# A decoder block on one core: two more pairs of gate and up tiles made by seven half-size products, the sums for it made earlier and those for the down projection later

## The reference

```
h = rms_norm(x, norm1);  proj = h @ w_in
o_diff = differential attention (4 heads);  o_nsa = compressed + selected + window attention (8 heads)
x = x + concat(o_diff, rms_norm(o_nsa)) @ w_out
h = rms_norm(x, norm2)
x = x + (silu(h @ w_gate) * (h @ w_up)) @ w_down        # w_gate, w_up: 1024 x 2816, w_down: 2816 x 1024
return rms_norm(x, final_norm)
```

## Time and profile before

| | |
|---|---|
| median of 3 runs | 668.09 us (666.64 to 669.31) |
| the profiled execution, its own time | 663.55 us |
| its span in the trace | 661.7 us |
| PE busy | 646.4 us, 98% of the span |
| DVE, ACT, POOL busy | 457.0, 348.7, 264.4 us |
| full tiles, from the first later chunk to the pairs | until 428.51 us |
| pairs | 428.51 to 548.72 us |
| down | from 548.72 us |

### The profile page before, as it was taken

How to read it: one execution, slowest core, us unless ns; L and a number is a source line. 1 busy time by engine, 2 the same in 40 slices (tenths; PEclk the granted TensorE clock), 3 DMA queues, 4 the chain that set the end, 5 groups by cost and what they waited for, 6 DMA issues and landing times.

```text
span 661.7 us, 11056 instructions
## 1 busy us (share of the span) xinstructions
PE 646.4 (98%) x3915; PEld 569.6 (86%) x3915; DVE 457.0 (69%) x929; ACT 348.7 (53%) x689; POOL 264.4 (40%) x158
## 2 busy tenths in 40 slices
PE   8999999999999799999999999999999999999996
PEld 7988988898899687888878888899999998888884
DVE  5435446555655777634579987669888798788894
ACT  7546446688564358725332353344444446655663
POOL 4766253684242431134356766444444320000222
PEclk9999999999999999999999999999999999999999
DMA  8979959469794982044699999977677858756553
GB/s 251 264 180 257 280 147 243 131 183 375 206 254 126 251 157 65 1 153 127 158 306 281 298 279 298 245 215 213 198 228 213 253 180 264 257 198 197 186 171 127
DMA packets 114774, 139.22 MB, mean 210 GB/s; under 512 B 5044, under 2 KB 74784, under 8 KB 114720
## 3 DMA queue, kind: packets, MB, share of 16 engines
q1 hardware_dynamic: 97880, 107.35, 50.6%
q0 software_dynamic: 14176, 26.64, 22.5%
q10 hardware_dynamic: 2664, 4.53, 1.9%
HBM read 132.19 MB, written 54.81 MB: 283 GB/s over the span
## 4 chain that ended last, share of the span: by engine, by line
PE 92%; DVE 2%; issue 2%; ACT 1%; POOL 1%; DMA 1%; POOLq 0%; ACTq 0%; DVEq 0%
PE bank L795 10%; PE bank L797 9%; PE bank L796 9%; PE bank L776 9%; PE bank L778 9%; PE bank L777 9%; PE bank L1107 6%; PE bank L1105 6%; PE bank L1106 6%; PE bank L948 6%; PE bank L924 3%; PE bank L908 2%; PE bank L909 2%; PE bank L987 1%; DMA causal<-in_c_causal_dram 1%
## 5 line engine op out<-in xcount | busy, mean ns | idle before, releaser
L728 POOL TENSOR_TENSOR w_lo<-raw,w_hi 128x1024 fp32r<-128x1024 f32 (+1 forms) x76 | 192.9, 2542 | 265.0 <-ACT w_hi L1148 264.2
L1148 ACT CAST w_hi<-raw 128x1024 fp32r<-128x1024 f32 (+1 forms) x141 | 144.2, 1028 | 141.4 <-PE bank L1107 51.8
L795 PE MATMUL bank<-xT_hi,w_hi 128*128 128x512 f32 x272 | 108.9, 400 | 0.8 <-POOL w_lo L728 0.5
L797 PE MATMUL bank<-xT_hi,w_lo 128*128 128x512 f32 x272 | 107.0, 394 | 0.0
L796 PE MATMUL bank<-xT_lo,w_hi 128*128 128x512 f32 x272 | 106.8, 392 | 0.0
L1617 DVE CUSTOM_DVE_ANT_0 bank<-bank,bias 128x128 f32<-128x128 f32 (+3 forms) x96 | 47.6, 497 | 74.5 <-PE bank L909 45.5
L1774 DVE TENSOR_TENSOR w_lo<-raw,w_hi 128x1024 fp32r<-128x1024 f32 x66 | 78.0, 1182 | 28.0 <-ACT w_hi L1148 28.0
L1229 ACT ACTIVATE E<-bank,nmax 128x128 f32<-128x128 f32 (+3 forms) x80 | 42.4, 530 | 38.3 <-DVE nmax L1617 37.5
L795 PEld LDWEIGHTS bank<-xT_hi,w_hi 128*128 128x128 f32 x272 | 51.2, 188 | 11.9 <-issue 1.2
L797 PEld LDWEIGHTS bank<-xT_hi,w_lo 128*128 128x128 f32 x272 | 51.1, 188 | 11.7
L796 PEld LDWEIGHTS bank<-xT_lo,w_hi 128*128 128x128 f32 x272 | 51.3, 188 | 9.7 <-issue 0.2
(11 more groups left out here) (280 smaller groups left out, 1615.7 us busy)
## 6 DMA issues: line engine op xcount, KB each, us to landing
raw<-mixed_sums SPq DMA_DIRECT2D x24, 512.0 KB, 4.4
raw<-in_w_gate_dram SPq DMA_DIRECT2D x22, 512.0 KB, 7.5
raw<-in_w_in_dram SPq DMA_DIRECT2D x20, 512.0 KB, 6.0
down_sums<-in_w_down_dram SPq DMA_DIRECT2D x20, 512.0 KB, 10.4
raw<-down_sums SPq DMA_DIRECT2D x20, 512.0 KB, 4.1
raw<-in_w_up_dram SPq DMA_DIRECT2D x16, 512.0 KB, 4.5
raw<-in_w_down_dram SPq DMA_DIRECT2D x15, 512.0 KB, 3.3
mixed_sums<-in_w_up_dram SPq DMA_DIRECT2D x12, 512.0 KB, 10.9
```

Source lines behind the costliest of these rows:

```text
L728: nc.gpsimd.tensor_tensor(wv_lo(k)[:, 0:n], raw[:, k % RAW_SLOTS, 0:n], wv_hi(k)[:, 0:n].bitcast(F32), ALU.subtract).then_inc(s_split, 1)
L795: nc.tensor.matmul(bank[:, :], hi, xT_hi[:, kt, :], start=kt == 0, stop=False)
L797: return nc.tensor.matmul(bank[:, :], lo, xT_hi[:, kt, :], start=False, stop=kt == KT - 1)
L1148: nc.scalar.copy(wv_hi(k)[:, 0:n], raw[:, k % RAW_SLOTS, 0:n]).then_inc(s_whi, 1)
```

## The change

`F0` goes from 10 to 6, so that four tiles of gate and up leave stage 1 and become two more pairs of stage 2 (6 pairs before, 8 now). The sums for the pairs grow from 24 to 32, so there are 56 in all, and their places are set anew. The ring of result banks gets another order, since the bank that gate and up used last must not be wanted first. POOL's loop now runs over the chunks of the down projection too, where six sums are made, and in each round it starts its sums last.

```diff
-F0 = 10
+F0 = 6
@@ plan_sums
-    for wides in ((0, 1), (2,)):
+    for wides in ((0, 1), (2, 3)):
@@ hymba_block
-    copy_at = [6 + i for i in range(10)] + [27 + i // 2 for i in range(14)]
-    copy_at += [n_fill + i for i in range(20)] + [n_fill + 2 * F0 + 4 + 10 * i for i in range(4)]
-    add_at = copy_at[0:16] + [30, 30, 30, 30, 31, 31, 31, 31] + copy_at[24:]
+    mixed0, down_from = n_fill + 2 * F0, n_fill + 2 * F0 + N_UNIT * N_PAIR
+    copy_at = [6 + i for i in range(10)] + [27 + i // 2 for i in range(14)] + [36] * 4
+    copy_at += [n_fill + i for i in range(12)] + [mixed0 + 3 + 5 * i for i in range(10)] + [down_from + 8 + 3 * i for i in range(6)]
+    add_at = copy_at[0:16] + [31] * 8 + [33] * 4 + copy_at[28:]
@@
-        RING = [ps[0], ps[6], ps[3], ps[4], ps[5], ps[2], ps[7], ps[1]]
+        RING = [ps[3], ps[4], ps[5], ps[2], ps[0], ps[6], ps[7], ps[1]]
@@ gpsimd
-            for k in range(down0):
+            for k in range(len(chunks)):
                 if not by_dve[k]:
                     split(k)
-                for i in [i for i in range(len(todo)) if add_at[i] == k]:
-                    add_sum(i)
                 if k == LAMBDA_AFTER:
...
                 if chunks[max(k - SPLIT_SLOTS, 0)][0] == "dk":
                     double_keys(job_of[chunks[k - SPLIT_SLOTS]])
+                for i in [i for i in range(len(todo)) if add_at[i] == k]:
+                    add_sum(i)
```

## The result

The changed kernel takes 678.7 us (median of 4 runs, 678.16 to 681.61), against 667.96 for the kernel before on the same chip (4 runs, 666.64 to 669.31): the ratio is 1.0174, with a 95% interval of 1.0145 to 1.0203. It is slower by 1.7%, and 3.7 us beyond the forecast's upper end.

What follows compares the result with a forecast made beforehand. PE, busy for 98% of the span, was taken as the bound. The terms -4.2 - 3.0 + 1.2 + 8.6 + 0.5 = +3.1 us gave 666.6 us on the profiled execution, 671.2 on the median (0.46% slower); range 664 to 675.

Steps and rivals of the forecast that it cites:

- Term 1: Exchanged work on PE: two pairs (40.07 us) in place of four tiles (44.24 us), -4.2 us.
- Term 2: Attention stage: POOL's split of chunk 31 moves earlier and PE's 3.03 us wait goes, -3.0 us (ends 0 and -3.4).
- Term 3: Last head's keys: their doubling meets four copies and lands later, so PE waits, +1.2 us (ends 0 and +3.8).
- Term 4: Passage into the pairs: PE waits 2.9 us at unit 2 and 5.8 at unit 4 for DVE's program, +8.6 us.
- low bound of 1.6 us: Passage into the pairs: the wait that remains if none of POOL's splits holds up DVE, 1.6 us.
- three blockings by POOL: Passage into the pairs: three POOL splits each hold up DVE operations with two SBUF inputs, adding 2.35 us each; chance 0.45.
- Term 5: Copies with their sums, ten in the pairs and six in down, cost PE little: +0.5 us (ends 0 and 3).
- lead of 6 us that hides it: Down: it may fall behind by 0.5 us per copy, 3 us over six, which its lead of 6 us hides.
- PE's clock falls in the wait: Rival, slower: PE's clock falls in the 5.8 us wait, 1.6 us per fall, 672.8 to 674.4 us; chance 0.18.
- transfers become the bound: Rival, in down or at the keys: terms 3 and 5 at their high ends, +5.1 us, 676 us; chance 0.10.

Runs made afterwards that it cites:

- k14: The changed kernel with eight full tiles and seven pairs (half of the exchange), half as large added sums and new copy places: 667.69 us.
- k1: The kernel before with only the attention stage's added sums moved behind both POOL splits: 662.04 us, ratio 0.9918.
- k11: The kernel before with 45 throw-away products ahead of the scores that wait at 221 us: 670.16 us.
- k15: The kernel before with 13 throw-away products ahead of the scores that wait at 221 us: 664.08 us, ratio 0.9965.
- k2: The changed kernel with the four copies and sums beside the last head's keys moved later, to chunk 37: 678.42 us.
- k3: The changed kernel with DVE's split of unit 4 moved ahead of the forms of tile 5: 679.23 us.
- k4: The changed kernel with 18 throw-away products on the free result bank ahead of PE's wait for unit 4: 679.62 us.
- k8: The changed kernel with the edits of k2 and k3, without the 24 copies and sums for down: 658.87 us, ratio 0.9866.
- k12: k8 with the 24 copies for down put back, but not their sums: 659.69 us.
- k17: The changed kernel with eight full tiles, seven pairs; two copies behind chunk 37, thirteen in the pairs, three in down: 667.52 us.
- k18: As k17, but four copies behind chunk 37 and eleven in the pairs, every four units: 660.62 us, ratio 0.9904.
- k5: The changed kernel with the last six copies and sums moved from down into the pairs: 681.69 us.
- k7: The changed kernel without the last six copies and sums, those of down: 673.6 us.
- k13: The changed kernel with down's six copies and sums six chunks apart instead of three: 680.51 us.
- k9: k3 with copies placed by idle transfer time, twelve of them and eight sums behind the last doubling of keys, none in down: 683.14 us.

## Why the prediction was wrong, by its own steps

**Term 1** (-4.2) was right: the units keep a pitch of 2.86, and k14 gives half of it.

**Term 2** (-3.0) was right as a wait (-2.9, k1). The baseline under it was not: I carried the profiled execution over to the median as a constant 4.54 us. k1, k11 and k15 show together that most of these microseconds are a fall of the clock behind this very wait, which most runs of before have and the profiled one lacks. On medians term 2 is worth 6.0, and the kernel after is 10.7 us above before where the profiles differ by 15.0. My remark that the 3.03 us wait left the next product at its usual length was true of one run.

**Term 3** (+1.2, ends 0 and 3.8) was mis-sized: the doubled keys land after 6.3 to 7.6 us, as reckoned, but the wait is 1.8 and the half clock behind it costs about 2.4 more.

**Term 4** (+8.6) was right as a mechanism and nearly in size: waits of 1.64 and 5.14 us against 2.9 and 5.8, 6.9 us with the little that unit 2 lost beside its wait, against 8.6. PE came 3.8 us later than I had it, DVE's chain only 2.8, which takes one microsecond off the waits. DVE's chain from `form_lo_a` (380.86) to the end of unit 4's split takes 25.8 us, and I had 26.2. My low bound of 1.6 us doesn't fit my own reason for it (18.4 plus 1.1 in a slot of 17.2 is 2.3); nothing hangs on it. The three blockings by POOL are there:

```profile
380.86 0.41 DVE L1781 TENSOR_TENSOR form_lo_a<-form_a,high_a 128x256 fp32r<-128x256 f32 x1
385.84 2.39 POOL L729 TENSOR_TENSOR w_lo<-raw,w_hi 128x1024 fp32r<-128x1024 f32 x1 [4.09 <-ACT w_hi L1149]
385.92 2.60 DVE L1834 TENSOR_TENSOR form_a<-gate_n,up_n 128x256 f32<-128x256 f32 x1
396.05 2.41 POOL L729 TENSOR_TENSOR w_lo<-raw,w_hi 128x1024 fp32r<-128x1024 f32 x1 [7.82 <-ACT w_hi L1149]
396.14 2.61 DVE L1838 TENSOR_TENSOR form_a<-gate_n,up_n 128x256 f32<-128x256 f32 x1
400.32 2.35 POOL L729 TENSOR_TENSOR w_lo<-raw,w_hi 128x1024 fp32r<-128x1024 f32 x1 [0.77 <-ACT w_hi L1149]
400.37 2.59 DVE L1844 TENSOR_TENSOR form_a<-form_a 128x256 f32<-128x256 f32 x1
405.49 1.21 DVE L1775 TENSOR_TENSOR w_lo<-raw,w_hi 128x1024 fp32r<-128x1024 f32 x1
```

Each takes the length of the POOL split beside it in place of 0.42. By the rule of the Trainium skill (GPSIMD Engine Reference, Specifications) that POOL contends with DVE instructions of two SBUF inputs, this is what had to come, and the trace agrees.

**Term 5** (+0.5, ends 0 and 3) is the step that failed. Stage 1 lost 2.3, the pairs 1.7 behind the waits of term 4, down 4.4: 8.4 us. What broke was the sentence "five units take 14.3 us for 7 transfers of 0.52 MB, 257 GB/s", and the same for down: it counts a sum as a transfer like another, by its megabytes. By the windows a sum takes 2.8 us of the engines, a copy 1.0. Three chunks of down with both need 3 x 1.58 + 3.8 = 8.5 us of the engines in the 8.4 that I gave them: no room, so that the lag grows. The share of 0.97 in down's first 68 us is this. (1.58 is 67.2 us over the 38.5 full chunks of down and four for the saved x.) The "lead of 6 us that hides it" is spent by 600 us. Nor did I look at stage 1, where sums meet the saving of x, as they did before without a wait. What I saw at 442 us before, one late cast without harm, was a single sum in ten units.

**The rivals.** "PE's clock falls in the wait" was true, twice, at 2.4 us each in place of 1.6; "transfers become the bound" was true as well, and got 0.10. I had them exclude each other, when a wait made by one brings the other. With both at their measured sizes (4.3 at the keys in place of 1.2, 8.4 in place of 0.5, 2.4 behind unit 4) my sum would be -4.2 - 3.0 + 4.3 + 8.6 + 2.4 + 8.4 = +16.5 on the profiled execution, where 15.0 were seen; term 4 was 1.7 too large. The 11.9 us by which my +3.1 fell short are 7.9 of term 5 and 4.8 of the clock with small ones, less these 1.7.

**Why no single repair helped.** k2, k3 and k4 each removed or shortened what they aimed at, and by the median lost it again. Their profiles have the loss in the next stretch short of transfers (k2 at 354 us, all three in down, 112.9 to 116.7 us), though with the scatter named above. k8 and k12 show it from the other side: the same repairs without the 24 sums are 19 to 20 us under the kernel after. That it is the sums and not the copies is shown by k12; that 11 of them fit into the seven pairs and 13 don't, by k17 and k18, for these spacings. Left open: why a sum takes three times a copy's time, and why a share of 0.88 is already too much in the pairs when 1.10 cost nothing in stage 1 before. A load that lands later can be enough, since the next may only start when one of three slots is free; no run changed a sum's form or the three slots of `raw`.

## What to carry to other kernels

Reckon transfers by the time that they keep the engines, not by bytes: take share times length of two windows that differ by one kind of transfer. An accumulating transfer in DRAM cost three plain ones here. When an edit removes a wait and the time stays, look for the next place where PE waits for a load, and compare several executions before you put a microsecond down to the edit.

Before adding one profile to the median of the runs, see whether both have the same mean clock; a difference of 0.01 was 4 us here.

## What the runs showed of the hardware that was not expected

- The granted clock was 0.50 (1.2 GHz) over 5 us behind waits of 1.8 and 5.1 us, and each time cost about 2.4 us; behind the first of these it was 0.64 to 0.74 over the same 5 us in k3, k5, k7 and k13; products of 256 columns then show as 0.41 us in place of 0.28. 36 throw-away matmuls in the longer wait kept it at 1.00 (k4), and 26 in the 3.0 us wait kept the mean at 0.997 or more in eight of eleven runs (k15). The Trainium skill (TensorE: Matmul & The Clock Gate, Part 1) calls the half clock the level to which an idle array returns; these rows agree. By the mean clocks of before's runs, the wait of 3.0 us brought the fall in most of them and not in others.
- By differences of share times length, an accumulating DRAM to DRAM transfer of 512 KB takes 2.8 us of all 16 engines, a copy 0.8 to 1.0, a load to SBUF 1.6 to 1.75 (k7, k8, k12 and after). Sums in a row start every 4 to 6 us (k9).
- The issue of a copy took 10.38 us of SP's time at a DMA share of 1.08, and a load issued 8 us before it landed after 19 us (after).
- Between 11 sums in 49 units, four units apart, and 13, three and a half apart, the loss goes from nothing to 8 us (pairs of 140.3 and 148.4 us, k18 and k17).
